# One core, three layers: the first modulation set fetched and used as scale, then shift, and five products of zeros ahead of the first product

## The chip, the core and the metric

The kernel runs on one core of a Trainium2 chip. A time is the device time of one execution in microseconds, and the metric is the median of the runs. A program writes each engine's instructions by hand: TensorE (PE) multiplies, VectorE (DVE), ScalarE (ACT) and GpSimd (POOL) do the rest, SyncE (SP) issues nearly all transfers, 16 DMA engines carry them. Semaphores are the only order between engines.

## What is computed

Two transformer layers and a third block run in sequence on 256 tokens of width 1024, beside a context of 256 tokens. The change touches the first step of the first layer. Cut from the reference:

```python
cond_lat, cond_ctx = silu(c), silu(c_ctx)
sh1, sc1, g1, sh2, sc2, g2 = split(cond_lat @ w_ada[i] + b_ada[i], 6)      # the same for the context
h = rms_norm(x, norm_gain[i, 0]) * (1.0 + sc1) + sh1
y = fftn(h.reshape(b, l, 8, 128), axes=(1, 3), norm='ortho').real          # tokens and 128 channels of a group
x = x + g1 * (y.reshape(b, l, D) @ w_out + b_out)
x = x + g2 * swiglu(rms_norm(x, ...) * (1.0 + sc2) + sh2)
```

Scale multiplies every channel of the spectrum over the tokens; shift is the same for all tokens, and so enters the spectrum only at frequency 0.

## The kernel before

**The front.** Four tiles of tokens (`xnat`) come first. ACT squares them, DVE scales the table of waves by the tokens' norms (`fs`, first tile pair ready at 9.5 us), and `spectrum(c, streams)` on TensorE gives the token spectrum of the 128 channels of chunk c, for stream 0 (latent) and stream 1 (context), in PSUM bank c. `scale_spectrum` (ACT for chunks 0, 2, 4, 6, 7, DVE for 1, 3, 5) multiplies it by gain x (1 + scale) into `Z`; `shift_spectrum` on DVE adds the shift at column 127. `channels(i)` takes the channel DFT of chunks 2i and 2i+1: the even half (columns 127 to 255, with the shift) by `cd`, the odd half (0 to 126) by `sd`. `nyquist(q)` takes the last frequency. ACT copies the results to `yh`, DVE puts the rest into `yl`, and `fnet_chunk(c)`, eight times 27 products, multiplies them by the output weights, split into `whi` (ACT) and `wlo` (DVE) after GpSimd folded them (`fold`).

**The modulation.** Weights come in blocks of 128 x 2048 numbers, one megabyte each, in the order of `STREAM`. A *set* is a stretch of modulation columns. `ada_rows(n, ks)` multiplies the condition by the blocks ks of set n (four products each, into bank 7), ACT copies the sum to `arow` (`arow_of`), `ada_cols(n)` turns it to columns on TensorE, and DVE adds the bias (`mods`) and, for the set of the scale, makes `amod` (`gains`). Set 0 holds shift and scale together: eight blocks of 128 rows and 2048 columns. Set 1 (g1) already comes as four blocks of 256 rows and 1024 columns (`TWO_DEPTHS`), whose turn is four products with a small table in place of four transposes. Set 2 has eight blocks.

**The transfers.** All blocks go through one queue, issued by SP in the order of `STREAM`, each as soon as its slot is free; the first 24 have eight slots (`ring`, `front_ring`). In this text B0 to B7 are the blocks of set 0, B8 is FNet block 0, B9 and B10 set 1, B11 FNet block 1, B12 and B13 set 1, B14 FNet block 2, B15 FNet block 3, B16 to B23 set 2, B24 the first FFN block; the tokens' own f32 copy `xT` (two megabytes) goes behind B14. B16 takes the slot of B8, free when block 0 is folded.

**TensorE's order** is written out by hand: spectrum products with the modulation blocks between them, then channel products, then the eight FNet chunks with the blocks of sets 1 and 2 between them (`MODS`). A product of f32 is two instructions in the trace.

## Time and profile before

| what | value |
|---|---|
| median of 3 runs | 1420.26 us (1420.25 to 1420.28) |
| profiled execution, own time | 1419.94 us |
| its span, first to last instruction | 1418.0 us |
| TensorE busy | 1379.8 us (97%) |
| VectorE, ScalarE, GpSimd busy | 56%, 37%, 5% |
| DMA, mean | 275 GB/s |

The busy share of TensorE is 97% but its ends are modelled, so pauses and pace are read from the timeline. The profiled execution is 0.32 us below the median; differences in the trace are put against its own time and then carried to the median. A row of the timeline gives start, length, engine, line, operation, output and inputs, count, and in brackets the idle time before it with what ended it.

### The profile page before, as it was taken

Reading aid. Unit: us, or ns where it says so; the run is one execution under the profiler, and the core shown is the slowest. Engines: PE = TensorE matmul, PEld = TensorE weight load, DVE = VectorE, ACT = ScalarE, POOL = GpSimd, SP = SyncE. Lnnn points to the kernel's source line nnn. Section 1 sums busy time; section 2 is a strip of 40 time slices with the busy share of each in tenths; the row PEclk is TensorE's granted clock in tenths of the full one; section 3 lists DMA queues with packets and bytes.
Section 4 is the critical chain, followed back from the end, with each engine's and each line's share of the span. In section 5 each row is a group of like instructions: output and inputs, shape, how many; then the busy total and the mean of one; then the engine's idle time right before and its main releaser. Section 6 shows DMA issues by size and latency. Waiting matters only on the chain.

```text
span 1418.0 us, 20093 instructions
## 1 busy us (share of the span) xinstructions
PE 1379.8 (97%) x8038; PEld 994.2 (70%) x8038; DVE 789.1 (56%) x1402; ACT 524.2 (37%) x1099; POOL 75.8 (5%) x74
## 2 busy tenths in 40 slices
PE   7999999999999999999999999999999999999987
PEld 4767887888887998888888998996444444443433
DVE  1978796665666886667788778684212112112113
ACT  2643222223444555445556666852111111111102
POOL 0600000000002141000000000010000000000000
PEclk9999999999999999999999999999999999999999
DMA  9958666764443332013687454478999999999995
GB/s 391 425 220 314 237 249 256 267 241 174 167 175 119 149 129 81 31 60 117 264 340 318 150 208 178 179 305 324 425 432 428 430 430 428 429 432 429 430 427 224
DMA packets 48130, 390.42 MB, mean 275 GB/s; under 512 B 5256, under 2 KB 6552, under 8 KB 9376
## 3 DMA queue, kind: packets, MB, share of 16 engines
q1 hardware_dynamic: 47408, 387.70, 68.1%
q8 instruction: 66, 1.08, 0.3%
q10 hardware_dynamic: 624, 1.37, 0.2%
q14 instruction: 32, 0.26, 0.1%
HBM read 388.01 MB, written 1.05 MB: 274 GB/s over the span
## 4 chain that ended last, share of the span: by engine, by line
PE 85%; DMA 8%; DVE 3%; ACT 2%; issue 1%; SPq 0%; DVEq 0%; ACTq 0%
PE twin L966 41%; PE twin L1627 19%; DMA ring<-in_wblk 6%; PE twin L1064 5%; PE twin L1065 3%; PE twin L1701 2%; DMA front_ring<-in_wblk 2%; PE twin L1610 2%; PE twin L1010 2%; PE twin L1480 2%; PE twin L1305 1%; PE twin L1241 1%; PE twin L1265 1%; DVE wlo L2388 1%; PE twin L886 1%
## 5 line engine op out<-in xcount | busy, mean ns | idle before, releaser
L2388 DVE TENSOR_TENSOR wlo<-ring,whi 128x512 fp32r<-128x512 f32 (+1 forms) x392 | 254.4, 697 | 64.7 <-ACT whi L1820 61.7
L1820 ACT ACTIVATE whi<-ring 128x512 fp32r<-128x512 f32 (+1 forms) x392 | 216.8, 611 | 106.7 <-PE twin L966 86.4
L966 PE MATMUL twin<-H,whi 128*128 128x512 f32 x700 | 216.3, 390 | 0.1
L966 PE MATMUL twin<-hsp,whi 128*128 128x512 f32 (+1 forms) x704 | 172.5, 337 | 1.8 <-DVE hsp L2587 0.9
L1627 PE MATMUL twin<-ring,xg 128*64 128x512 f32 x696 | 158.3, 597 | 8.4 <-DMA ring<-in_wblk 8.0
L966 PEld LDWEIGHTS twin<-H,whi 128*128 128x128 f32 x700 | 130.8, 188 | 30.1 <-issue 2.5
L966 PE MATMUL twin<-H,wlo 128*128 128x512 f32 x350 | 136.2, 389 | 0.0
L966 PEld LDWEIGHTS twin<-hsp,whi 128*128 128x128 f32 x704 | 120.7, 190 | 17.0 <-DVE wlo L2388 1.7
L1064 PE MATMUL twin<-H,whi 128*128 128x512 f32 x350 | 124.2, 400 | 0.5 <-DVE H L2485 0.2
L966 PE MATMUL twin<-hsp,wlo 128*128 128x512 f32 (+1 forms) x352 | 118.3, 336 | 0.0
L1627 PEld LDWEIGHTS twin<-ring,xg 128*64 128x64 f32 x696 | 48.0, 137 | 97.0 <-issue 88.2
L1627 PE MATMUL twin<-ring,xT 128*64 128x512 f32 x456 | 102.0, 595 | 2.5 <-DMA ring<-in_wblk 2.0
L3174 DVE TENSOR_TENSOR rst<-rst,twin 128x512 f32<-128x512 f32 x16 | 11.0, 688 | 166.4 <-issue 161.2
L1065 PE MATMUL twin<-H,wlo 128*128 128x256 f32 x350 | 98.3, 281 | 0.0
L966 PE MATMUL twin<-whi,Hh 128*128 128x256 f32 x304 | 88.3, 291 | 0.0
L966 PE MATMUL twin<-wlo,Hh 128*128 128x256 f32 x304 | 85.9, 283 | 0.0
L966 PE MATMUL twin<-whi,Hl 128*128 128x256 f32 x304 | 85.9, 283 | 0.0
L3189 DVE SCALAR_TENSOR_TENSOR outs<-twin,tiny,outs 128x512 fp32r<-128x512 f32 x32 | 24.0, 751 | 104.6 <-ACT outs L2282 52.8
L1064 PEld LDWEIGHTS twin<-H,whi 128*128 128x128 f32 x350 | 65.8, 188 | 17.6 <-DVE H L2485 0.6
L2587 DVE TENSOR_TENSOR hsp<-hid,hsp 128x512 fp32r<-128x512 f32 (+1 forms) x88 | 49.1, 563 | 50.5 <-ACT hsp L1928 50.5
L1928 ACT ACTIVATE hsp<-hid 128x512 fp32r<-128x512 f32 (+1 forms) x88 | 45.5, 524 | 84.6 <-PE twin L966 84.6
L1627 PEld LDWEIGHTS twin<-ring,xT 128*64 128x64 f32 x456 | 32.1, 137 | 62.4 <-issue 62.3
(428 smaller groups left out, 2375.6 us busy)
## 6 DMA issues: line engine op xcount, KB each, us to landing
ring<-in_wblk SPq DMA_DIRECT2D x213, 1024.0 KB, 6.1
ring<-in_wblk SPq DMA_DIRECT2D x56, 2048.0 KB, 30.6
front_ring<-in_wblk SPq DMA_DIRECT2D x12, 1024.0 KB, 19.1
small<-in_wblk SPq DMA_DIRECT2D x10, 1024.0 KB, 26.4
tmp<-in_wblk SPq DMA_DIRECT2D x9, 1024.0 KB, 23.8
ring<-in_wblk SPq DMA_DIRECT2D x12, 512.0 KB, 18.8
xnat<-in_xnat SPq DMA_DIRECT2D x4, 512.0 KB, 6.7
xT<-in_xin SPq DMA_DIRECT2D x1, 2048.0 KB, 23.4
```

The lines of the kernel that those rows point to most:

```text
L966: t = e.matmul(out, a, b, start=start and n == 0, stop=stop and n == 2)
L1010: e.matmul(out[:, r], ws[x][:, k, m * P:(m + 1) * P], y[:, i, r], start=k == 0 and n == 0, stop=k == KC - 1 and n == 2, skip_group_check=True)
L1064: e.matmul(b[:, :].rearrange("p (x n) -> p x n", x=2), w[0], FHB[1][:, :, k, :], start=start, stop=stop, skip_group_check=True)
L1065: return e.matmul(b[:, 0:L], w[1], FH[1][0][:, k, :], start=False, stop=stop, skip_group_check=True)
L1480: t = e.matmul(wout_bank(b, m)[:, m * L:(m + 1) * L], ws[i][:, k, m * P:(m + 1) * P], XM[j][:, k, :], start=k == 0 and (m == 0 or b == 3) ...
L1610: t = e.matmul(gather_bank(q, j)[:, i * 256:(i + 1) * 256], h2[n % 2][:, n // 2, c * P:(c + 1) * P], Gs[:, n // 2, :], start=n == 0, stop= ...
L1627: t = e.matmul(like(out[64 * i:64 * i + 64, :], rows), lhs(kcs + kk, i), rows, start=start and kk == 0, stop=stop and kk == 3)
L1701: t = e.matmul(acc(c), osp[:, part_, c * P:(c + 1) * P], Sw[:, p % 2, :], start=p == 0 and part_ == 0 and c % 2 == 0, stop=p == NP - 1 and ...
L1820: e.activation(hi, w, ACT.Copy).then_inc(*s_hi.up(m, h))
L1928: e.activation(hsp[:, k % nsp, 0, 0:n], hid[:, k, 0:n], ACT.Copy).then_inc(*s_hph.up(layer, half, k))
L2388: e.tensor_tensor(lo, w, hi.bitcast(F32), ALU.subtract).then_inc(*s_lov.up(m, h))
L2587: e.tensor_tensor(hsp[:, k % nsp, 1, 0:n], hid[:, k, 0:n], hsp[:, k % nsp, 0, 0:n].bitcast(F32), ALU.subtract).then_inc(*s_hpl.up(layer, h ...
```

## The change

The four blocks of scale columns (256 rows, 1024 columns each) now come first, as set 0, the four of the shift columns follow, as a set of its own named "shift" with bank 4 for its rows. Both are turned as set 1 is. ACT's and DVE's scaling of Z waits for set 0 alone. The products of the channel DFT are split: the odd halves wait for the scaled Z, the even halves for the shifted one. Spectrum 4 goes first on TensorE, since bank 4 is wanted for the shift's rows. The late blocks of sets 1 and 2, and the turn of set 1, are placed behind other chunks. GpSimd first clears `rst`, and TensorE multiplies it by itself five times into bank 6, which nobody reads, before its first real product. The host lays the blocks out accordingly. The counts of semaphores that follow from it are left out below.

```diff
@@ -93,12 +93,12 @@
...
 WEIGHED.update({(2, 1 + i): (("fin", 1, 2 * i + 4), 2 * i + 4) for i in range(7)})
-PE_ROWS = {0: range(8), 1: range(4), 2: range(8), 6: range(2), 7: range(1), 8: range(1)}
-ADA0 = {0: (0, 2), 1: (2, 1), 2: (3, 2), "g2": (5, 1)}
-ORDER = [0, 1, 2, "g2", 3, 4, 5, 6, 7, 8]
+PE_ROWS = {0: range(4), "shift": range(4), 1: range(4), 2: range(8), 6: range(2), 7: range(1), 8: range(1)}
+ADA0 = {0: (1, 1), "shift": (0, 1), 1: (2, 1), 2: (3, 2), "g2": (5, 1)}
+ORDER = [0, "shift", 1, 2, "g2", 3, 4, 5, 6, 7, 8]
 BEFORE = dict(zip(ORDER[1:], ORDER[:-1]))
-MOD_STREAMS = {n: 2 if n in (0, 1, 2, "g2", 3) else 1 for n in ORDER}
-TWO_DEPTHS = (1, "g2")
+MOD_STREAMS = {n: 2 if n in (0, "shift", 1, 2, "g2", 3) else 1 for n in ORDER}
+TWO_DEPTHS = (0, "shift", 1, "g2")
 G2 = 4
@@ -474,7 +476,7 @@
...
         def modulated(layer, s, chunk6):
-            return s_mod.at(3 * layer + chunk6 // 2 if layer else (0, 0, 1, 2, 2, "g2")[chunk6], s)
+            return s_mod.at(3 * layer + chunk6 // 2 if layer else ("shift", 0, 1, 2, 2, "g2")[chunk6], s)
@@ -495,8 +497,8 @@
...
         s_a0 = signal("fnet_scales", [(0,)])
-        s_d1 = signal("dft_tokens", [(c,) for c in range(KC)])
-        ACT_SCALED, DVE_SCALED = (0, 2, 4, 6, 7), (1, 3, 5)
+        s_d1 = signal("dft_tokens", [(c,) for c in (4, 0, 1, 2, 3, 5, 6, 7)])
+        ACT_SCALED, DVE_SCALED = (4, 0, 2, 6, 7), (1, 3, 5)
         s_za = signal("spectrum_scaled_act", [(c,) for c in ACT_SCALED])
@@ -635,7 +637,10 @@
...
         def turned_rows(n):
-            return bank[{0: 7, 6: 5}.get(n, 6)]
+            return bank[{0: 7, "shift": 4, 6: 5}.get(n, 6)]
+
+        def rows_bank(n):
+            return bank[4 if n == "shift" else 7]
@@ -872,19 +879,21 @@
...
             def ada_rows(n, ks):
-                layer, s = SETS[n]
+                layer, s = (0, 0) if n == "shift" else SETS[n]
                 for k in ks:
-                    tag = ("ada", layer, s, k)
+                    tag = ("ada", layer, s, k + 4 if n == "shift" else k)
                     w = block_of(tag)
                     e.wait_ge(*landed(tag))
-                    if k == 0 and n:
-                        e.wait_ge(*s_arow.at(n - 1))
+                    if k == 0 and n == "shift":
+                        e.wait_ge(*s_za.at(4))
+                    elif k == 0 and n:
+                        e.wait_ge(*s_arow.at(BEFORE[n]))
                         if n == 1:
...
                     for g in range(4):
-                        depth = 2 * k + g // 2 if n == 1 else k
-                        t = e.matmul(bank[7][32 * g:32 * g + 32, :], cact[:, 1 if layer == 2 else 0, depth, :], w[:, g * 512:(g + 1) * 512],
-                                     start=k == 0, stop=k == (3 if n == 1 else 7), skip_group_check=layer == 2)
+                        depth = 2 * k + g // 2 if n in TWO_DEPTHS else k
+                        t = e.matmul(rows_bank(n)[32 * g:32 * g + 32, :], cact[:, 1 if layer == 2 else 0, depth, :], w[:, g * 512:(g + 1) * 512],
+                                     start=k == 0, stop=k == (3 if n in TWO_DEPTHS else 7), skip_group_check=layer == 2)
                     t.then_inc(*s_adam.up(n, k))
@@ -972,7 +981,7 @@
...
                     for t2 in range(2):
-                        if c == 0:
+                        if c == 4:
                             e.wait_ge(*s_fs.at(2 * s + t2))
@@ -980,12 +989,17 @@
...
-            def channels(i):
-                e.wait_ge(*s_dc.at(2 * i + 1))
-                for table, r, n0, n1 in ((cd, EVEN, 127, 256), (sd, ODD, 0, 127)):
-                    for j in range(2):
-                        t = e.matmul(streams(spectrum_bank[i][64 * j:64 * j + 64, r]), table, Z[:, 2 * i + j, :, n0:n1], start=True, stop=True)
-                t.then_inc(*s_d2.up(i))
+            def channels(i, r):
+                if r == ODD:
+                    for c in (2 * i, 2 * i + 1):
+                        e.wait_ge(*(s_za if c in ACT_SCALED else s_zv).at(c))
+                else:
+                    e.wait_ge(*s_dc.at(2 * i + 1))
+                table, n0, n1 = (sd, 0, 127) if r == ODD else (cd, 127, 256)
+                for j in range(2):
+                    t = e.matmul(streams(spectrum_bank[i][64 * j:64 * j + 64, r]), table, Z[:, 2 * i + j, :, n0:n1], start=True, stop=True)
+                if r == EVEN:
+                    t.then_inc(*s_d2.up(i))
@@ -1016,43 +1030,50 @@
...
-            for c in range(4):
+            e.wait_ge(*s_zero.at("warm"))
+            for _ in range(5):
+                e.matmul(bank[6][:, :], rst[:, 0, 0:P], rst[:, 0, :], start=True, stop=True)
+            for c in (4, 0, 1, 2, 3):
                 spectrum(c, (0,))
+            spectrum(4, (1,))
+            e.wait_ge(*s_cond.at("c2"))
+            ada_rows(0, (0,))
             spectrum(0, (1,))
-            e.wait_ge(*s_cond.at("c2"))
-            ada_rows(0, range(2))
             spectrum(1, (1,))
+            ada_rows(0, (1,))
+            spectrum(2, (1,))
             ada_rows(0, (2,))
-            spectrum(2, (1,))
+            spectrum(3, (1,))
+            spectrum(5, (0,))
             ada_rows(0, (3,))
-            spectrum(3, (1,))
-            spectrum(4, (0,))
-            ada_rows(0, (4,))
-            spectrum(4, (1,))
-            ada_rows(0, (5,))
-            spectrum(5, (0,))
-            ada_rows(0, (6,))
             spectrum(5, (1,))
-            ada_rows(0, (7,))
-            spectrum(6, (0,))
             e.wait_ge(s_cons, 16)
             ada_cols(0)
-            spectrum(6, (1,))
-            spectrum(7)
-            channels(0)
-            channels(1)
+            spectrum(6)
+            spectrum(7, (0,))
+            ada_rows("shift", (0,))
+            spectrum(7, (1,))
+            ada_rows("shift", (1, 2))
+            channels(0, ODD)
+            ada_rows("shift", (3,))
+            channels(1, ODD)
+            ada_cols("shift")
+            channels(2, ODD)
+            channels(3, ODD)
+            channels(0, EVEN)
+            channels(1, EVEN)
             nyquist(0)
-            channels(2)
+            channels(2, EVEN)
             ada_rows(1, range(1))
-            channels(3)
+            channels(3, EVEN)
             nyquist(1)
             ada_rows(1, range(1, 2))
-            MODS = {0: (1, range(2, 4)), 3: (2, range(1)), 4: (2, range(1, 3)), 5: (2, range(3, 5)), 6: (2, range(5, 6))}
+            MODS = {0: (1, range(2, 3)), 1: (1, range(3, 4)), 3: (2, range(1)), 4: (2, range(1, 2)), 5: (2, range(2, 4)), 6: (2, range(4, 6))}
             for c in range(KC):
...
                     ada_rows(*MODS[c])
-                if c == 1:
+                if c == 2:
                     ada_cols(1)
@@ -1823,7 +1844,7 @@
...
                     e.wait_ge(*s_adat.at(BEFORE[i]))
-                e.activation(arow[:, :], bank[7][:, :], ACT.Copy).then_inc(*s_arow.up(i))
+                e.activation(arow[:, :], rows_bank(i)[:, :], ACT.Copy).then_inc(*s_arow.up(i))
@@ -1884,6 +1905,7 @@
...
                 scale_spectrum(c)
+            arow_of("shift")
             for i in range(4):
@@ -1903,7 +1925,7 @@
...
                 e.activation(streams(tmp[:, c % 4, :])[:, :, 0:129:128], streams(even)[:, :, 0:129:128], ACT.Identity, bias=col("fb", c)).then_inc(*s_fna.up(c, "ends"))
-                if c == 0:
+                if c == 1:
                     arow_of(1)
@@ -2308,6 +2330,7 @@
         def pool(e):
+            e.memset(rst[:, 0, :], 0.0).then_inc(*s_zero.up("warm"))
             e.memset(cact[:, :, :, :], 0.0).then_inc(*s_zero.up("cact"))
@@ -2541,14 +2564,11 @@
...
             e.wait_ge(*s_a0.at(0))
-            scale_spectrum(1)
-            shift_spectrum(0)
-            shift_spectrum(1)
-            scale_spectrum(3)
-            shift_spectrum(2)
-            shift_spectrum(3)
-            scale_spectrum(5)
-            for c in range(4, KC):
+            for c in DVE_SCALED:
+                scale_spectrum(c)
+            mods("shift")
+            e.wait_ge(*s_mod.at("shift", 1))
+            for c in range(KC):
                 shift_spectrum(c)
@@ -3323,9 +3343,10 @@
...
             m = w["w_ada_2"][0] if t[1] == 2 else w["w_ada"][t[1]]
-            if t[1] == 0 and t[2] in (1, 3):
-                a = 2048 if t[2] == 1 else 5120
-                wblk[n] = m[t[3] * 2 * P:(t[3] + 1) * 2 * P, a:a + BW // 2].reshape(2, P, BW // 2).transpose(1, 0, 2).reshape(P, BW)
+            if t[1] == 0 and t[2] != 2:
+                a = {0: 0 if t[3] >= 4 else 1024, 1: 2048, 3: 5120}[t[2]]
+                k = t[3] % 4
+                wblk[n] = m[k * 2 * P:(k + 1) * 2 * P, a:a + BW // 2].reshape(2, P, BW // 2).transpose(1, 0, 2).reshape(P, BW)
             else:
...
                 wblk[n] = m[t[3] * P:(t[3] + 1) * P, a:a + BW]

```

Three places of the engines' order, each row an instruction group of the program (line, operation, output and inputs, output shape, count of products). TensorE from its first product on, before:

```order
L977 MATMUL twin<-fs,xnat 128x256 x10
L886 MATMUL twin<-ring,small 32x512 x8
L977 MATMUL twin<-fs,xnat 128x256 x2
L886 MATMUL twin<-ring,small 32x512 x4
L977 MATMUL twin<-fs,xnat 128x256 x2
```

and in the changed kernel:

```order
L1035 MATMUL twin<-rst 128x512 x5
L986 MATMUL twin<-fs,xnat 128x256 x12
L895 MATMUL twin<-ring,small 32x512 x4
L986 MATMUL twin<-fs,xnat 128x256 x4
L895 MATMUL twin<-ring,small 32x512 x4
```

Five products of zeros stand first; the first modulation block comes two spectrum products later and alone. (L977 and L986 are `spectrum`, L886 and L895 `ada_rows`.) TensorE from the last blocks of set 0 to the channel products, before:

```order
L886 MATMUL twin<-front_ring,small 32x512 x4
L977 MATMUL twin<-fs,xnat 128x256 x2
L916 MATMUL twin<-cons,small 128x128 x4
L977 MATMUL twin<-fs,xnat 128x256 x6
L987 MATMUL twin<-Z,dft 64x258 x2
L987 MATMUL twin<-Z,dft 64x254 x2
L987 MATMUL twin<-Z,dft 64x258 x2
L987 MATMUL twin<-Z,dft 64x254 x2
L992 MATMUL twin<-Z,dft 32x258 x4
```

and in the changed kernel:

```order
L923 MATMUL twin<-cons,small 128x8 x4
L986 MATMUL twin<-fs,xnat 128x256 x6
L895 MATMUL twin<-front_ring,small 32x512 x4
L986 MATMUL twin<-fs,xnat 128x256 x2
L895 MATMUL twin<-front_ring,small 32x512 x8
L1000 MATMUL twin<-Z,dft 64x254 x2
L895 MATMUL twin<-front_ring,small 32x512 x4
L1000 MATMUL twin<-Z,dft 64x254 x2
L923 MATMUL twin<-cons,small 128x8 x4
L1000 MATMUL twin<-Z,dft 64x254 x4
L1000 MATMUL twin<-Z,dft 64x258 x4
L1006 MATMUL twin<-Z,dft 32x258 x4
```

The turn (L916, now L923) of the scale stands ahead of the shift blocks, a second turn behind them, and odd channel products (64x254) lie around it. DVE from the modulation to the first split, before:

```order
L2400 TENSOR_TENSOR mod<-twin,cols 128x16 x2
L2468 SCALAR_TENSOR_TENSOR amod<-mod,cols 128x8 x2
L2532 TENSOR_SCALAR Z<-twin,amod 128x256 x2
L2541 SCALAR_TENSOR_TENSOR Z<-mod,Z 128x2 x2
L2532 TENSOR_SCALAR Z<-twin,amod 128x256 x2
```

and in the changed kernel:

```order
L2423 TENSOR_TENSOR mod<-twin,cols 128x8 x2
L2491 SCALAR_TENSOR_TENSOR amod<-mod,cols 128x8 x2
L2555 TENSOR_SCALAR Z<-twin,amod 128x256 x6
L2423 TENSOR_TENSOR mod<-twin,cols 128x8 x2
L2564 SCALAR_TENSOR_TENSOR Z<-mod,Z 128x2 x8
```

The three scalings stand together, and all eight shifts behind the second `mod`.

## Rows read from the trace of the kernel before

**Rows 1.** The page, part 4: the chain that ended last, by engine

```profile
PE 85%; DMA 8%; DVE 3%; ACT 2%; issue 1%; SPq 0%; DVEq 0%; ACTq 0%
```

**Rows 2.** Chain of waits, 0 to 200 us: start, us, what

```profile
6.43 25.16 DMA front_ring<-in_wblk
...
33.76 0.45 PE twin L916 x4
...
35.34 3.75 ACT Z L1881 x10
...
90.62 46.63 PE twin L966 x204
```

**Rows 3.** Timeline of TensorE, first 80 us

```profile
9.54 7.21 PE L977 MATMUL twin<-fs,xnat 128*128 128x256 f32 x20 [9.54 <-DVE fs L2509]
...
31.63 1.06 PE L886 MATMUL twin<-front_ring,small 128*32 128x512 f32 x8 [0.82 <-DMA front_ring<-in_wblk]
...
43.85 0.39 PE L1010 MATMUL twin<-yh,whi 128*128 128x258 f32 x1
...
45.41 0.39 PE L1010 MATMUL twin<-yh,whi 128*128 128x258 f32 x1 [0.20 <-DVE yl L2555]
...
47.75 1.92 PE L886 MATMUL twin<-front_ring,small 128*32 128x512 f32 x16
49.60 0.39 PE L1010 MATMUL twin<-yh,whi 128*128 128x258 f32 x1
...
52.94 0.96 PE L914 MATMUL twin<-cons,small 128*128 128x8 f32 x8
53.75 0.37 PE L1010 MATMUL twin<-yh,whi 128*128 128x258 f32 x1
...
60.39 1.06 PE L886 MATMUL twin<-ring,small 128*32 128x512 f32 x8
...
79.63 1.02 PE L924 MATMUL twin<-hid,cons 128*128 128x512 f32 x2
```

**Rows 4.** Busy time from 15 to 80: engines, then PEclk, DMA share, GB/s

```profile
15.00:80.00 65.00, 63.97 (x474) 42.25 (x473) 38.73 (x75) 25.57 (x56) 25.92 (x16) 1.00 1.01 424
```

**Rows 5.** Spectrum products (L977) in two stretches: PE, PEld, PEclk, DMA share, GB/s

```profile
9.50:14.80 5.30, 5.26 (x12) 4.21 (x13) 1.00 1.02 426
14.80:16.60 1.80, 1.80 (x9) 1.37 (x7) 1.00 1.00 423
```

**Rows 6.** SP's issue of B16, then of B24, each with its time to landing

```profile
38.93 0.33 SPq L841 DMA_DIRECT2D ring<-in_wblk  x1
...
DMA to landing us min/median/max: 19.5/19.5/19.5
...
65.03 0.43 SPq L841 DMA_DIRECT2D ring<-in_wblk  x1
...
DMA to landing us min/median/max: 13.1/13.1/13.1
```

**Rows 7.** Timelines of ACT (one row) and DVE around the modulation

```profile
32.77 0.60 ACT L1826 ACTIVATE small<-twin 128x512 f32<-128x512 f32 x1 [18.38 <-PE twin L886]
...
34.24 0.26 DVE L2400 TENSOR_TENSOR mod<-twin,cols 128x16 f32<-128x16 f32 x2 [18.59 <-PE twin L916]
34.44 0.86 DVE L2468 SCALAR_TENSOR_TENSOR amod<-mod,cols 128x8 f32<-128x8 f32 x2
...
38.47 0.82 DVE L2541 SCALAR_TENSOR_TENSOR Z<-mod,Z 128x2 f32<-128x2 f32 x4
```

**Rows 8.** Timeline of GpSimd: first clear, fold of blocks 0 and 3

```profile
0.73 0.52 POOL L2311 MEMSET small<- 128x512 f32 x1 [0.29 <-POOLq L3296]
...
33.93 4.97 POOL L2327 TENSOR_TENSOR fold<-ring 128x512 f32<-128x512 f32 x4 [31.53 <-DMA ring<-in_wblk]
...
56.11 8.52 POOL L2327 TENSOR_TENSOR fold<-front_ring 128x512 f32<-128x512 f32 x4 [1.33 <-DMA front_ring<-in_wblk]
```

**Rows 9.** Busy time of the stretch 960 to 980, PEclk third from the end

```profile
960.00:980.00 20.00, 19.57 (x130) 16.34 (x130) 10.61 (x41) 9.13 (x19) 0.00 (x0) 0.91 0.78 306
```

More of the change, by code:

```diff
@@ L459, in program @@
         s_cond = signal("conditions_ready", [("c0",), ("c2",)])
-        s_zero = signal("cleared", [("cact",), ("wny",), ("eps",), ("pick",), ("lx",), ("sT",)])
+        s_zero = signal("cleared", [("warm",), ("cact",), ("wny",), ("eps",), ("pick",), ("lx",), ("sT",)])
         events = []
@@ L465, in program @@
                 events.append([("sum", "g2"), ("rows", "g2")])
+            if n == 1:
+                events += [[("shift", k)] for k in range(3)] + [[("shift", 3), ("rows", "shift")]]
             mine = [[(n, k)] for k in PE_ROWS.get(n, ())] + [[("sum", n)]] * (layer > 0)
@@ L785, in used @@
                         e.wait_ge(*s_adv.at("g2", tag[3]))
+                    elif tag[1:3] == (0, 0) and tag[3] >= 4:
+                        e.wait_ge(*s_adam.at("shift", tag[3] - 4))
                     else:
```

## The prediction

> **What bounds the kernel now.** The page comes first: TensorE holds 85% of the chain that ended last, DMA 8% [rows 1]. The change touches the first 60 us only, so the chain of waits of that stretch is next. It hangs on one transfer until 31.59 us, block B7, the eighth of the first modulation set; from the first layer's FFN on it is TensorE [rows 2]. TensorE's own timeline shows what lies between [rows 3]: products without a pause from 9.54 to 30.81, a pause of 0.82 for B7, and then again no pause until chunk 0 of the FNet output product at 43.85, in which it waits once more (45.41, for the low part of the spectrum). A normal chunk takes 3.34 (49.60 to 52.94), chunk 0 takes 3.90 (43.85 to 47.75). So TensorE is the bound from 31.6 on, and up to there it runs only 0.82 ahead of the transfers. Underneath, the DMA engines are full: their share is 1.01 of the stretch from 15 to 80 [rows 4], so no transfer of it can land sooner; only their order can change, and each set keeps its eight megabytes.
>
> One more thing is in TensorE's front. Its first 12 matmul instructions (each product of f32 is two) take 5.26 us, the next 9 take 1.80, though the forms are the same and the granted clock reads 1.00 in both [rows 5]. Start to start that is 0.43 against 0.216 us: the engine ran at 1.2 GHz when it came out of idling and at 2.4 GHz from 14.8 us. What this costs is 12 x (0.427 - 0.216) = 2.53 us. In the kernel before most of it would not pay back: all but 0.82 us of TensorE's lead is waiting for B7 anyway if it comes early.
>
> **The change part by part.**
>
> *Scale first.* B7, now the last shift block, lands at 31.6 as before [rows 2]. B3, now the last scale block, is four blocks of 1.05 MB ahead of it, at 424 GB/s [rows 4] some 9.9 us, so at about 21.7. TensorE's own pace in the new order, from rows 3 at full clock (four spectrum instructions 0.86 and up to 0.2 for the change of kind, a modulation block 1.0, a turn of eight 0.81): it starts at 9.54, has done 24 spectrum instructions at 14.9, scale blocks and their neighbours at 23.8, the turn at 25.7, and reaches the last shift block at about 32.9. That is 1.3 later than B7 lands. So the wait for B7 (0.82) is gone, and TensorE alone sets the time. The scaling of Z, which began 3.7 us after B7's products before (31.63 to 35.34) [rows 2, 3], begins at about 27, on ACT and DVE, beside spectrum products.
>
> *The second turn.* One turn of 4 instructions, 0.45 [rows 2], becomes two of 8; one such turn takes 0.81 (52.94 to 53.75) [rows 3]. Added on TensorE: 2 x 0.81 - 0.45 = 1.17 us. The weight blocks themselves cost the same: eight blocks, four products each. Behind the shift blocks a new chain stands: copy of the rows on ACT, turn, mod on DVE (0.26), eight shifts of Z (four took 0.82, so 1.6 in all); the copy itself takes 0.60 [rows 7]. TensorE covers the copy with the odd products of pair 1 and the mod and the first shifts with the odd products of pairs 2 and 3 (1.0 us). The old chain had these steps too, with amod (0.86) and the scaling between them; I take 0.3 us of waits left, bounds 0 (all covered) and 1.1 (copy and mod bare, 0.6 + 0.26 and their handing over).
>
> *Channel products in halves.* The same instructions; the odd half needs no shift. No cost beyond a seam or two. The yh, whi, yl, wlo chain on ACT and DVE starts about 1.8 earlier and TensorE arrives at chunk 0 about 2 earlier; the folded weights of chunk 0 are ready at 38.9 (33.93 + 4.97) [rows 8] and do not bind. The 0.56 us that chunk 0 loses now (3.90 - 3.34) goes, since the Z scaling no longer fills both engines up to 39 us; bounds 0 and 0.56.
>
> *Five products of zeros.* They need a memset of 512 columns, 0.52 us from 0.73 on [rows 8], so they start at about 1.3. At the low clock one instruction of 512 columns takes twice 0.427, so ten take 8.5 us at most; if the clock rises after the same 5.3 us of work as in the trace, at 6.6, they end at 8.3, before 9.54, when the scaled waves of the first tile are there. They then cost nothing, and the main products start at 2.4 GHz: 2.53 us less. The pause between them and 9.54 is 1.2 us; the nearest one in the rows is the 0.82 at 30.8, behind which a modulation block takes 1.06 like the one at 60.39 [rows 3]. The other clears on GpSimd come 0.5 later, and nobody waits for them before 13 us.
>
> The Trainium skill, "TensorE: Matmul & The Clock Gate", Part 1, says the default state of the clock is the throttled one and that activity of the engine releases it; rows 5 agree. By that rule zeros count as work like any other, and the sum stays. The same part warns that the point of the rise varies from run to run; then some of the 2.53 us could be lost in one execution, by the next step less than half a microsecond of time.
>
> *Sum up to the end of chunk 3.* Before, the modulation block behind chunk 3 starts at 60.39. Off it: 0.82 + 2.53 + 0.56 = 3.91; on it: 1.17 + 0.3 = 1.47. The two late blocks of set 1 and its turn are only moved within this stretch. TensorE would arrive at 60.39 - 2.44 = 57.95.
>
> *What is late next.* There it needs B16, the first block of set 2. Its DMA is issued at 38.93, when the fold of FNet block 0 frees its slot, and lands 19.5 later, at 58.43 [rows 6]. The fold waits for B8's landing (33.93), not for TensorE, so the issue time does not move, and neither does the landing with full DMA engines. So TensorE waits about 0.5 us and starts B16 at 58.47 in place of 60.39: **1.92 us** are left. Behind it the new list spreads the blocks of set 2 over later chunks: at 424 GB/s a block of 1.05 MB follows every 2.5 us, so B17 lands at about 60.9 and is taken after chunk 4 at about 62.8, B18 and B19 land at 63.4 and 65.9 and are taken after chunk 5 at about 67.2. None binds. DVE and ACT have slack behind chunk 6, and chunk 7 ends 1.92 sooner than 79.63 [rows 3]. B24, the first FFN block, lands at 65.03 + 13.1 = 78.1 [rows 6]; ACT would want it at 78.4, so it just does not bind.
>
> *To the end.* From there on TensorE carries the chain, and the transfers wait for slots that TensorE, ACT and DVE free, up to the expert stage, whose fill also hangs on them. I see nothing that gives the time back: the shift passes whole. Profiled execution: 1419.94 - 1.92 = 1418.02; the median of the runs stands 0.32 above it, so 1420.26 - 1.92 = **1418.3**.
>
> **The rivals.**
>
> *The zeros do not lift the clock* (slower). The mechanism: zeros, or the pause of 1.2 us behind them, leave the engine at 1.2 GHz until about 14.8. Then 2.53 us come back, and the ten instructions, all at 0.855, end at 9.85, which delays the first real product by 0.3. TensorE arrives behind chunk 3 at 57.95 + 2.83 = 60.8 and is 0.4 later than before: 1420.7. It decides from 2.44 us of loss on. For it: nothing in the rows shows products of zeros. Against it: the rise comes while the engine works, whatever is in it.
>
> *B16 does not hold* (faster still). If it lands sooner or TensorE's sum is right and the block is there, 2.44 us: 1417.8. Against it: the DMA share of 1.01.
>
> *The low parts hold.* Folding one block took 4.97 us when DVE mostly read PSUM and 8.52 when DVE worked from SBUF beside it [rows 8]. DVE now splits weights earlier, beside the fold of block 1. If chunk 2 or chunk 6 finds its low weights missing by 1 us, what is left is about 0.9: 1419.4. The Trainium skill, "GPSIMD Engine Reference", section "Key points", says that GpSimd shares its SBUF interfaces with VectorE and contends with instructions of two SBUF inputs; rows 8 agree.
>
> *The clock at a later stage.* The granted clock is 0.91 in the stretch 960 to 980 [rows 9]. A start 1.9 us sooner may lose or gain one stretch at half clock somewhere, priced by the front's at 2.5: 1420.8 or 1415.8.
>
> **How the numbers follow.** Forecast (1417.8 to 1418.8, by the waits of 0 to 1.1 and B16's hold): 0.60. B16 not holding 0.08, low parts 0.12, zeros 0.09, later clock stretch 0.09 (half each way), anything worse 0.02. The range leaves out the later gain and half of the slow ends: 1417.3 to 1420.7. This kernel's measurement can tell about 0.2%, 2.84 us. Faster than that (below 1417.42) needs the later gain, or B16 early by more than 0.5 with no wait left: 0.08. Slower than 1423.1 needs zeros and a later loss together: 0.03. Within: 0.89.
>
> **What would show it.** Products of the first spectrum chunks at 0.216 from 9.5 on; no pause before the last shift block; the last shift block's products at about 33; chunk 0 at about 41.7 and 3.4 long; a pause of about 0.5 before the block behind chunk 3, which starts at 58.4 to 58.5; the first FFN products 1.9 sooner. It would be wrong if those first products still took 0.43, if B16 landed elsewhere than at 58.4, or if the gap between the two traces changed anywhere behind 90 us.

## The result and the profile after

| what | before | changed |
|---|---|---|
| median of the runs taken side by side (14 each) | 1419.74 us (1418.13 to 1421.23) | 1421.59 us (1419.06 to 1424.53) |
| ratio to before, 95% interval | | 1.0018 (1.0011 to 1.0025) |
| profiled execution, own time | 1419.94 us | 1424.53 us |
| its span | 1418.0 us | 1422.3 us |
| start of the first layer's FFN products (chain) | 90.62 us [rows 2] | 93.33 us |

The changed kernel is slower: by 1.9 us between the two medians, by 2.6 by the ratio, with an interval of 1.6 to 3.5. The forecast was 1.9 us faster. The shares of the chain that ended last look much as before [rows 1] and do not tell why; the timelines of the first 70 us do.

**The front does what was forecast, with one exception.** TensorE's timeline of the changed kernel (start, length, engine, line, operation, output and inputs, shape, count, idle time before it and what ended it):

```profile
1.31 6.17 PE L1035 MATMUL twin<-rst 128*128 128x512 f32 x10 [1.31 <-POOL rst L2333]
9.31 5.45 PE L986 MATMUL twin<-fs,xnat 128*128 128x256 f32 x24 [1.83 <-DVE fs L2532]
...
32.61 1.06 PE L895 MATMUL twin<-front_ring,small 128*32 128x512 f32 x8
...
37.70 0.66 PE L1000 MATMUL twin<-Z,dft 128*64 128x258 f32 x4 [0.57 <-DVE Z L2564]
...
42.53 0.39 PE L1024 MATMUL twin<-yh,whi 128*128 128x258 f32 x1
...
46.15 1.06 PE L895 MATMUL twin<-front_ring,small 128*32 128x512 f32 x8
```

The 24 spectrum instructions take 5.45 us, 0.22 each, where the first 12 of before took 0.43 each [rows 5]: the ten instructions of zeros take 6.17 us, 0.85 from start to start at first (1.2 GHz) and 0.43 at the end (2.4 GHz), and the real ones find the 2.4 GHz level, in spite of 1.83 us of idling between them. The last shift block is worked on at 32.61 with no pause ahead of it. Behind it the spectrum waits 0.57 us for the eight shifts of DVE (L2564), and chunk 0 starts at 42.53, 1.3 earlier than before [rows 3], where I had 41.7.

**Then the gain is lost at one place.** TensorE again, from the turn of set 1 on. The first fence is the changed kernel, the second before, where the turn stood one chunk earlier [rows 3]:

```profile
54.87 0.96 PE L923 MATMUL twin<-cons,small 128*128 128x8 f32 x8
...
59.08 1.06 PE L895 MATMUL twin<-ring,small 128*32 128x512 f32 x8
62.55 0.56 PE L1024 MATMUL twin<-yh,whi 128*128 128x258 f32 x1 [2.40 <-DVE wlo L2411]
62.90 0.42 PE L1024 MATMUL twin<-yl,whi 128*128 128x258 f32 x1
...
67.47 1.07 PE L895 MATMUL twin<-ring,small 128*32 128x512 f32 x8
```

```profile
61.38 0.39 PE L1010 MATMUL twin<-yh,whi 128*128 128x258 f32 x1
```

At 59.08 TensorE is 1.31 ahead of before (60.39). Chunk 4 should follow at 60.1; it waits 2.40 us for the low part of its weights, starts at 62.55, 1.17 *behind* before (61.38), and its first products, some 15 of them, take 0.215 us from start to start (62.90 to 63.12 and so on), where those of chunk 0 take 0.12. Here is why DVE is late, changed kernel, timelines of DVE and of GpSimd:

```profile
55.86 0.24 DVE L2423 TENSOR_TENSOR mod<-twin,cols 128x8 f32<-128x8 f32 x2 [3.79 <-PE twin L923]
56.14 5.75 DVE L2550 SCALAR_TENSOR_TENSOR xT<-tmp,mod,xT 128x256 f32<-128x256 f32 x4
61.81 2.48 DVE L2411 TENSOR_TENSOR wlo<-fold,whi 128x512 fp32r<-128x512 f32 x4
```

```profile
55.98 5.63 POOL L2350 TENSOR_TENSOR fold<-front_ring 128x512 f32<-128x512 f32 x4 [1.73 <-DMA front_ring<-in_wblk]
```

and the same of DVE before:

```profile
54.74 1.67 DVE L2527 SCALAR_TENSOR_TENSOR xT<-tmp,mod,xT 128x256 f32<-128x256 f32 x4
56.33 2.49 DVE L2388 TENSOR_TENSOR wlo<-fold,whi 128x512 fp32r<-128x512 f32 x4
```

DVE adds the FNet result times g1 to `xT` (L2550), and that needs the modulation of set 1, hence its turn. Before, the turn came behind chunk 1, DVE began the four additions at 54.74 and was in the last of them when GpSimd came to fold block 3 (56.11, [rows 8]). Now the turn comes behind chunk 2, the additions begin at 56.14, and the fold began at 55.98, when its block had landed. The additions begin 1.4 us apart in place of 0.4, one with each fold instruction. Behind them in DVE's queue stand the four `wlo` of chunk 4, for which TensorE waits. Before, the order of arrival was the other way round, and it was GpSimd that was held up: 8.52 us for the fold [rows 8], which nobody on the chain waits for; it takes 5.63 now.

The chain of waits of the changed kernel tells the same in one line each (start, us, what):

```profile
56.14 5.75 DVE xT L2550 x4
...
62.55 4.64 PE twin L1024 x24
...
93.33 6.77 PE twin L975 x28
```

**A second loss on top.** Busy time of the changed kernel (PE, PEld, DVE, ACT, POOL, then PEclk, DMA share, GB/s):

```profile
60.00:65.00 5.00, 2.60 (x15) 2.45 (x12) 4.96 (x9) 0.63 (x1) 1.61 (x2) 0.76 1.01 424
65.00:70.00 5.00, 5.00 (x38) 4.03 (x37) 4.34 (x10) 4.09 (x10) 0.00 (x0) 0.90 1.01 426
...
930.00:935.00 5.00, 5.00 (x22) 4.60 (x22) 2.41 (x4) 2.60 (x8) 1.47 (x2) 0.50 0.56 197
```

Behind the 2.40 us of waiting the granted clock falls (0.76, then 0.90), and chunk 4 with its Nyquist products takes 4.92 us from its start to the block behind it (62.55 to 67.47). In the kernel before it takes 3.40, and in a second trace of the changed kernel (e7, below) 3.43. That is 1.5 us more, so the stretch costs 1.31 + 1.17 + 1.52 = 4.0 us in this execution, and the FFN starts 2.71 late. The offset between the two traces stays at about 2.7 up to 920 us and jumps to 5.7 where the granted clock is 0.50 (930 to 935; 1.00 there before). It falls by 1.0 where the kernel before has a half-clock stretch of its own (at 967), and the spans end 4.3 apart.

### The profile page after: what moved, and what is told of

Read it like the earlier page. It is cut to its first block, busy times and chain, and to the rows that moved or that the text cites. A ratio compares the mean times of both kernels' runs of the same rounds, so it can differ in the third digit from the quotient of the medians.

```text
span 1422.3 us, 20149 instructions
## 1 busy us (share of the span) xinstructions
PE 1389.6 (98%) x8060; PEld 999.3 (70%) x8060; DVE 792.3 (56%) x1404; ACT 525.2 (37%) x1100; POOL 72.7 (5%) x75
## 3 DMA queue, kind: packets, MB, share of 16 engines
q8 instruction: 66, 1.08, 0.3%
HBM read 388.01 MB, written 1.05 MB: 274 GB/s over the span
## 4 chain that ended last, share of the span: by engine, by line
PE 87%; DMA 6%; DVE 4%; ACT 2%; issue 1%; SPq 0%; DVEq 0%; ACTq 0%
PE twin L975 41%; PE twin L1648 19%; DMA ring<-in_wblk 6%; PE twin L1085 5%; PE twin L1086 3%; PE twin L1722 2%; PE twin L1631 2%; PE twin L1024 2%; PE twin L1501 2%; PE twin L895 1%; PE twin L1326 1%; PE twin L1262 1%; PE twin L986 1%; PE twin L1286 1%; DVE wlo L2411 1%
```

## The experiments

Two theories. **A**, the collision: DVE's additions lose their place ahead of GpSimd's fold because the turn of set 1 was moved; the waiting and all the loss come from that. **B**, the new front itself: less slack between fetched blocks, DVE and ACT behind because of the second turn and the eight shifts, so that the loss would stay wherever the turn is. (The expectations below use B for other rivals, and each says which: in e1 stretches of half clock at later stages, in e3 no effect at all, in e7 a wait that does not come back.) Each ratio is uncertain by some 1.3 us either way, so the verdicts rest on the start of the first layer's FFN products in the trace, and the ratios are read beside it. Three groups (the first four, the next three, the last two) have each their own runs of before beside them.

**e1_turn_back.** The changed kernel with the turn of set 1 and its blocks back where they were.

```
-            MODS = {0: (1, range(2, 3)), 1: (1, range(3, 4)), 3: ...
+            MODS = {0: (1, range(2, 4)), 3: ...
-                if c == 2:
+                if c == 1:
                     ada_cols(1)
...
-                if c == 1:
+                if c == 0:
                     arow_of(1)
```

> The changed kernel with one part undone: both late blocks of set 1 stand behind chunk 0 and its turn behind chunk 1, as before the change. Theory A (collision): in the changed kernel DVE's four additions to xT start at 56.14 us, the moment GpSimd starts to fold block 3, and take 5.75 us in place of 1.67; the low weights of chunks 4 and 5 come late for it, TensorE waits 2.4 us and runs chunk 4 partly at 1.2 GHz. With the turn back the additions start at 53.7 (xT lands then) and are over before the fold: no wait before chunk 4, FFN's long run of products starts at about 88.7 to 89.2 (90.6 before, 93.3 changed), time 1.5 to 2 us below the kernel before. Theory B (the loss is not in the front but in stretches of half clock at later stages, which come or stay away by chance of the start): the median stays within 1 us of the changed kernel's, 1.5 to 2 above before, wherever the FFN starts.

Measured: 1418.33 us against 1419.08 of before, ratio 0.9997 (0.9988 to 1.0006). DVE's timeline, TensorE's block behind chunk 3, and the chain:

```profile
53.60 2.24 DVE L2550 SCALAR_TENSOR_TENSOR xT<-tmp,mod,xT 128x256 f32<-128x256 f32 x4 [0.42 <-DVE mod L2423]
...
58.86 1.06 PE L895 MATMUL twin<-ring,small 128*32 128x512 f32 x8
...
89.09 11.07 PE twin L975 x47
```

The additions take 2.24 us (the first of them 1.05, beside the last fold instruction of block 2) and are over at 55.8, TensorE does not wait for chunk 4, and the FFN starts at 89.09: 1.53 sooner than before and 4.24 sooner than in the changed kernel. The front alone would have left the wait there. Half clock at later stages would have left the median 1.5 to 2 above before; it is 0.75 below, less than the 1.5 to 2 expected by A and inside what the ratio leaves open.

**e2_fold_waits.** The turn stays late; GpSimd is told to wait with the fold of block 3 until the four additions are through.

```
+                    if b == 3:
+                        e.wait_ge(*s_fnx.at(1, 1))
```

> The changed kernel, its order untouched, but GpSimd folds block 3 only when DVE has finished the first two chunks' additions to xT. Theory A: the additions take 1.7 us (56.1 to 57.8) again, the low weights of block 2 are there at about 60.3, TensorE waits at most 0.3 us before chunk 4 and the FFN starts at about 89; time 1 to 2 us below the kernel before. Rival C (the additions are slow for another reason, such as the landing of xT or full transfers into SBUF): they still take over 4 us and the time stays at the changed kernel's. Rival D (the fold is needed at once): the wait is only moved to chunk 6, and the gain is under 1 us.

Measured: 1418.38 us against 1419.08, ratio 0.9994 (0.9985 to 1.0003). DVE, GpSimd, chain:

```profile
56.36 1.67 DVE L2552 SCALAR_TENSOR_TENSOR xT<-tmp,mod,xT 128x256 f32<-128x256 f32 x4
...
58.20 8.06 POOL L2352 TENSOR_TENSOR fold<-front_ring 128x512 f32<-128x512 f32 x4 [3.71 <-DVE xT L2552]
...
89.54 10.60 PE twin L975 x45
```

With the turn as late as in the changed kernel, the additions take 1.67 again as soon as GpSimd is not beside them, and the FFN starts 1.08 sooner than before. So it is the meeting that costs, not the late turn as such. The fold begins 2.2 late and takes 8.06, and nobody on the chain waits for it: rival D of the expectation, a wait moved to chunk 6, falls too, since TensorE has no pause ahead of chunk 6 (69.95).

**e3_before_late_turn.** The kernel before, with nothing of the change but the turn of set 1 behind chunk 2.

```
-                if c == 1:
+                if c == 2:
                     ada_cols(1)
```

> The kernel before with one part of the change alone: the turn of set 1 behind chunk 2 in place of chunk 1. TensorE does the same products. Theory A: DVE's four additions start at about 57.9, inside the fold of block 3 (56.1 on), and take 4 to 6 us; low weights of chunk 4 come at 64 or later, TensorE waits 2 to 3 us there: FFN start 92.5 to 94, time 2 to 4 us above before. Theory B: nothing that can be measured, within 0.5 us of before.

Measured: 1420.85 us against 1419.08, ratio 1.0010 (1.0001 to 1.0019). DVE, TensorE's chunk 4, chain:

```profile
55.87 4.83 DVE L2527 SCALAR_TENSOR_TENSOR xT<-tmp,mod,xT 128x256 f32<-128x256 f32 x4
...
62.43 0.39 PE L1010 MATMUL twin<-yh,whi 128*128 128x258 f32 x1 [2.55 <-DVE wlo L2388]
...
91.70 8.34 PE twin L966 x35
```

One changed number makes the old kernel slower and shows the same wait (2.55 for 2.40) and the same stretched additions (4.83). The FFN starts 1.08 late, less than the 1.9 to 3.4 expected, because TensorE was 1.6 ahead here at the block behind chunk 3 (58.81 against 60.39): it took B7 0.8 earlier in this execution, and chunk 0 took 3.42 in place of 3.90. Behind the wait it was late by 1.08: 2.7 us went. Without that head start the additions would have begun later still, so 1.1 us is, by this argument, the least that the one line costs. One thing does not fit a plain order of arrival: the first addition began at 55.87, 0.12 *ahead* of the fold (55.99), and was through in 0.48; the other three were caught (1.5 each).

**e4_before_zeros.** The kernel before with the clear and the five products of zeros, and nothing else.

```
+            e.wait_ge(*s_zero.at("warm"))
+            for _ in range(5):
+                e.matmul(bank[6][:, :], rst[:, 0, 0:P], rst[:, 0, :], start=True, stop=True)
...
+            e.memset(rst[:, 0, :], 0.0).then_inc(*s_zero.up("warm"))
```

> The kernel before with the memset and the five products of zeros alone. The prediction said that TensorE's lead over the eighth block is waited away: the first spectrum products run at 0.216 us from 9.5 on, the pause before the last block of set 0 grows from 0.82 to about 3.3 us, chunk 0 starts at 43.85 as before, and the time is that of the kernel before within 0.3 us. Rival: a pause of 3.3 us before the last block lets the clock fall again (the granted clock under 1.00 behind it, products at 0.43), and the time is 1 to 3 us above before.

Measured: 1419.39 us against 1419.08, ratio 0.9999 (0.9989 to 1.0009). TensorE's timeline and the chain:

```profile
9.51 4.58 PE L977 MATMUL twin<-fs,xnat 128*128 128x256 f32 x20 [1.00 <-DVE fs L2513]
...
15.96 1.06 PE L886 MATMUL twin<-ring,small 128*32 128x512 f32 x8 [0.88 <-DMA ring<-in_wblk]
...
29.14 1.06 PE L886 MATMUL twin<-front_ring,small 128*32 128x512 f32 x8 [1.20 <-DMA front_ring<-in_wblk]
...
90.65 9.45 PE twin L966 x40
```

The 20 instructions take 4.58 in place of 7.21 [rows 3], and the 2.6 us are waited away again. I had expected one pause of 3.3 before B7; there are five smaller ones (0.88, 0.30, 0.30, 1.20, 0.21), and the granted clock stays at 1.00 through them. In the old order the zeros are worth nothing (+0.03 at the FFN); the prediction had said that most would not pay back.

**e5_one_shift.** e1, and the eight shifts of Z as one instruction of 128 x 16 in place of eight of 128 x 2.

```
-            def shift_spectrum(c):
...
-                e.scalar_tensor_tensor(Z[:, c, :, 127:128], shift, math.sqrt(2.0), Z[:, c, :, 127:128], ALU.mult, ALU.add).then_inc(*s_dc.up(c))
+            def shift_spectrum():
...
+                shift = mod[:, 0, :].rearrange("p (s x) -> p s x", s=2)[:, :, 0:KC]
+                at_zero = Z[:, :, :, 127:128].rearrange("p c s n -> p s (c n)")
+                e.scalar_tensor_tensor(at_zero, shift, math.sqrt(2.0), at_zero, ALU.mult, ALU.add).then_inc(*s_dc.up(0))
```

> The version with the turn of set 1 back behind chunk 1, and the eight additions of the shift to Z joined in one instruction of 128 x 16 numbers. Theory A (a DVE instruction that reads two operands in SBUF waits for the GpSimd instruction that runs, so each of a row of short ones pays up to one fold of 1.27 us): the eight cost 3.3 us in the runs so far, one costs at most 1.4, the wait of TensorE before the even products (0.57) and the short ones behind it go, chunk 0 starts about 0.8 to 1.2 sooner than at 42.6, and the block B16, landing at 58.4, takes back all but 0.3 to 0.5 of it: FFN start 88.6 to 88.8, time 1.5 to 2.5 us below before. Rival E (the additions are slow because each waits for its own predecessor, with GpSimd or without): one instruction costs 0.15 to 0.3 and chunk 0 starts 1.5 or more sooner.

Measured: 1417.94 us against 1419.55, ratio 0.9987 (0.9979 to 0.9996): faster than before. DVE, TensorE, chain:

```profile
35.75 0.73 DVE L2563 SCALAR_TENSOR_TENSOR Z<-mod,Z 128x16 f32<-128x16 f32 x1
...
41.73 0.39 PE L1024 MATMUL twin<-yh,whi 128*128 128x258 f32 x1
...
58.45 1.06 PE L895 MATMUL twin<-ring,small 128*32 128x512 f32 x8 [0.43 <-DMA ring<-in_wblk]
...
88.71 11.49 PE twin L975 x49
```

This is the trace that the prediction described, but of another kernel, with two parts of the change made otherwise: chunk 0 at 41.73 (41.7), a wait of 0.43 for B16 behind chunk 3 (0.5), its products at 58.45 (58.47), the FFN 1.91 sooner (1.92). Rival E of the expectation, that the shifts are slow with GpSimd or without, falls with e6, where eight of them take 0.66 with the fold over.

**e6_no_zeros.** e1 without the five products of zeros; the clear stays.

```
-            for _ in range(5):
-                e.matmul(bank[6][:, :], rst[:, 0, 0:P], rst[:, 0, :], start=True, stop=True)
```

> The version with the turn of set 1 back, without the five products of zeros. The prediction's step: with scale first TensorE has no lead left, so the half clock of the first products now costs its full 2.5 us: first spectrum products at 0.43, the last shift block taken at about 35 in place of 32.6, chunk 0 at about 45, the block behind chunk 3 at about 61.3 with no wait for its landing. Its FFN start is then 91.3 to 92 (89.1 with zeros, 90.6 before), and the time 0.7 to 1.5 us above before. If the rival holds that the zeros are worth nothing here as they were in the kernel before, FFN start stays at 89.1 to 89.5.

Measured: 1420.22 us against 1419.55, ratio 1.0004 (0.9995 to 1.0012). TensorE's first rows, DVE's shifts, the chain:

```profile
9.58 8.10 PE L986 MATMUL twin<-fs,xnat 128*128 128x256 f32 x24 [9.58 <-DVE fs L2530]
...
35.54 1.06 PE L895 MATMUL twin<-front_ring,small 128*32 128x512 f32 x8
...
38.69 0.66 DVE L2562 SCALAR_TENSOR_TENSOR Z<-mod,Z 128x2 f32<-128x2 f32 x8
...
91.05 9.01 PE twin L975 x38
```

The FFN starts 1.96 later than in e1 and 0.43 later than before. In the new order the zeros are needed: without them TensorE reaches the last shift block at 35.54. Of the 2.9 us lost there (32.61 in the changed kernel, 32.64 in e1), about 1.0 comes back, a little more than expected (91.3 to 92). One source is the shifts: they fall behind GpSimd's fold of block 0 here (it ends at 38.2) and take 0.66 us, where they take 3.26 beside it in the changed kernel.

The second meeting happens here too, although the turn is early. DVE:

```profile
55.17 2.72 DVE L2548 SCALAR_TENSOR_TENSOR xT<-tmp,mod,xT 128x256 f32<-128x256 f32 x4
57.82 5.84 DVE L2409 TENSOR_TENSOR wlo<-fold,whi 128x512 fp32r<-128x512 f32 x4
```

The fold of block 3 begins at 56.04 and catches the fourth addition and three of the `wlo`. TensorE does not wait for them: it comes to chunk 4 at 61.82 here, and behind chunk 3 it is 1.96 later than in e1 (60.82 against 58.86), the same as at the FFN. So the 1.96 is the zeros' worth and holds nothing of this meeting.

**e7_changed_again.** The changed kernel, unchanged, beside e5 and e6.

> The changed kernel as it is, beside the others on one chip. Theory A: the wait of about 2.4 us before chunk 4 recurs in every execution, since it hangs on GpSimd's fold beginning before DVE's additions. What the clock does behind it may differ: either chunk 4 runs partly at 1.2 GHz (FFN start near 93.3) or not (near 91.7); the stretch at half clock near 930 us of the first trace stays away or stands elsewhere. Theory B: the wait itself is gone in this execution.

Measured: 1422.0 us against 1419.55, ratio 1.0015 (1.0007 to 1.0024), the first result again. Chain, DVE and the window behind the wait:

```profile
56.19 5.72 DVE L2550 SCALAR_TENSOR_TENSOR xT<-tmp,mod,xT 128x256 f32<-128x256 f32 x4
...
60.00:65.00 5.00, 2.63 (x24) 2.44 (x21) 4.97 (x8) 0.63 (x1) 1.63 (x2) 1.00 1.00 421
...
91.84 8.33 PE twin L975 x35
```

The stretched additions and the wait are there again to a few hundredths, the half clock behind it is not: granted clock 1.00, FFN at 91.84 in place of 93.33. So 1.22 us late is what the collision alone leaves of the change, and the other 1.5 of the first trace come with the half clock. That they belong to one execution alone is not shown: the medians stand 1.9 and 2.5 above before, and the granted clock over a whole execution is lower in this kernel (mean of its 26 executions 0.9963, of the 85 of before beside the experiments 0.9974, of e3's 11, with the same wait, 0.9976). Some loss at half clock therefore recurs; where it lies, two traces do not tell.

**e8_late_turn_one_shift.** One question was left: with chunk 0 at 41.7 instead of 42.5, as I had forecast, the additions would begin ahead of the fold. Is it the slow shifts that tip the order over (theory C), or is the late turn bad in itself (D)? The changed kernel with e5's one shift instruction and nothing else.

> The changed kernel with its late turn of set 1, and only the eight shifts of Z made one instruction. In the changed kernel the additions to xT begin 0.16 us behind the fold of block 3 (56.14 and 55.98); with chunk 0 at 41.7 in place of 42.5 they should begin at about 55.3, ahead of the fold by 0.7. Theory C: the slow shifts are what tips the order over. Then DVE, being under way, keeps its lead as before the change (there the fold came 1.37 us into DVE's run): additions in 1.6 to 1.7 us, no wait ahead of chunk 4, B16 waited for until 58.45, FFN products at 88.7, median about 1.9 us below before. Theory D: being ahead by less than a microsecond does not help, the fold gets in after the second addition (in the old kernel with the late turn the fold came 0.12 us after the first addition began and did get in): two additions at 0.4, two at 1.5, additions done at about 59.2, the weights of chunk 4 at about 60.0 to 61, chunk 4 0.4 to 1.5 late, FFN at 89.1 to 90.2.

Measured: 1420.27 us against 1419.29, ratio 1.0008 (0.9999 to 1.0018). DVE, GpSimd, TensorE, chain:

```profile
55.21 2.73 DVE L2550 SCALAR_TENSOR_TENSOR xT<-tmp,mod,xT 128x256 f32<-128x256 f32 x4
57.87 5.82 DVE L2411 TENSOR_TENSOR wlo<-fold,whi 128x512 fp32r<-128x512 f32 x4
...
56.09 6.44 POOL L2350 TENSOR_TENSOR fold<-front_ring 128x512 f32<-128x512 f32 x4 [1.76 <-DMA front_ring<-in_wblk]
...
61.42 0.39 PE L1024 MATMUL twin<-yh,whi 128*128 128x258 f32 x1 [0.72 <-DVE wlo L2411]
...
90.95 9.23 PE twin L975 x39
```

C falls. The additions begin 0.88 ahead of the fold, three of the four take their 0.4 us, the fold gets in ahead of the fourth, and now the four `wlo` of chunk 4 meet it instead: 5.82 us in place of 2.5. TensorE waits inside chunk 4, several times up to 0.7 us each. The FFN starts at 90.95, 0.33 later than before. That is D's mechanism at more than D's price (89.1 to 90.2), since I had let the weights go unhindered. So neither arrival tried with the late turn is a good one: 0.88 ahead of the fold, the weights are caught; 0.16 behind it, all four additions.

**e9_one_shift_again.** e5 unchanged, beside e8.

> The kernel of the run with the turn of set 1 back and one shift instruction, unchanged, beside it. If its gain is not of one chip and one session: FFN products at 88.7 (to 0.2), ratio between 0.998 and 0.9996 again. If the first ratio was luck: 0.9997 or above.

Measured: 1417.72 us against 1419.29, ratio 0.9990 (0.9980 to 0.9999). Chain:

```profile
88.75 11.28 PE twin L975 x48
```

Against e8 it differs in the place of the turn and of one block alone: 2.20 us at the FFN. The gain of e5 is there again, 1.87 us in the trace.

All in one table; the offset is the start of the FFN products against 90.62 of before, the last column the interval of the ratio in microseconds of before's median:

| kernel | offset in the trace | interval of the runs |
|---|---|---|
| changed | +2.71 | +1.6 to +3.5 |
| e7, changed again | +1.22 | +1.0 to +3.4 |
| e1, turn of set 1 back | -1.53 | -1.7 to +0.9 |
| e2, fold waits | -1.08 | -2.1 to +0.4 |
| e3, before with late turn | +1.08 | +0.1 to +2.7 |
| e4, before with zeros | +0.03 | -1.6 to +1.3 |
| e5, e1 with one shift | -1.91 | -3.0 to -0.6 |
| e6, e1 without zeros | +0.43 | -0.7 to +1.7 |
| e8, changed with one shift | +0.33 | -0.1 to +2.6 |
| e9, e5 again | -1.87 | -2.8 to -0.1 |

Every offset lies within the interval of its runs. In all ten traces the offset is still the same at 560 us, to 0.03. Behind that the traces part: e1, e2 and e9 gain 0.9 more between 560 and 900 us, which no run here explains, and stretches at half clock, in other places in each execution, add or take 1 to 3 us. What the first 90 us give or take passes to the end only within what the runs can resolve.

## Why the prediction was wrong

**Where it failed.** The step that failed is "The two late blocks of set 1 and its turn are only moved within this stretch". I counted the turn's own 0.81 us on TensorE, found it unchanged, and did not follow who waits for it: ACT's copy, DVE's `mod`, the four additions to `xT`, and behind them in the same queue the weights of chunk 4. The prediction gives no reason for taking the move as free; all it says of these queues is "DVE and ACT have slack behind chunk 6". At chunk 4 DVE had 1.7 us of additions and 2.5 of weights to do, in a place that it shared with GpSimd's fold. The move delayed the additions by 1.40 (54.74 to 56.14), which put them from just ahead of the fold to just behind its start. Price: 5.75 - 1.67 = 4.1 us on DVE, 2.4 of waiting on TensorE. e1 and e2 remove it by either of its two partners, e3 makes it in the old kernel, e7 repeats it, and e8 shows that the forecast would have failed at this step even with every other term right: +0.33 where I had -1.92.

**The rival that was nearest.** "The low parts hold" was the right mechanism with the right rows (the fold of 4.97 and of 8.52), but I looked for it at chunks 2 and 6, gave it 1 us and a chance of 0.12, and had GpSimd as the one that is slowed. Rows 8 show the direction in which the collision is harmless. The harmful one, DVE held up by a fold that came first, could nearly have been worked out before: the fold of block 3 begins at 56.11 [rows 8]; the turn comes a chunk later, 52.94 + 3.34 [rows 3], less the 2.4 that I had TensorE ahead, so at 53.9 at best; the additions follow 1.27 behind a turn in the changed kernel (54.87 to 56.14), so at 55.2 (55.21 in e8); four of them and four `wlo` are 4.0 us of work (54.74 to 58.74 before), most of it behind 56.1. The Trainium skill, "SBUF — State Buffer", section "Who interferes with whom", says it outright: "Issue order, not op shape, decides who blocks." The traces agree in the main: with DVE ahead, four additions take 1.67 and the fold 8.52; with the fold ahead, it takes 5.63 and the additions 5.75. How far ahead is enough, they answer unevenly (last section).

**The shifts** (a term of the right kind, too small). I had eight at 1.6 us, from four at 0.82 [rows 7], and 0.3 us of waits. They took:

```profile
35.77 3.26 DVE L2564 SCALAR_TENSOR_TENSOR Z<-mod,Z 128x2 f32<-128x2 f32 x8
```

beside this row of GpSimd:

```profile
33.84 4.95 POOL L2350 TENSOR_TENSOR fold<-ring 128x512 f32<-128x512 f32 x4 [30.98 <-DMA ring<-in_wblk]
```

It is the same collision at another place. The new order sets the shifts at 35.8, inside the fold of block 0 (33.84 to 38.8); alone they take 0.66 (e6), as one instruction 0.73 (e5). It put chunk 0 at 42.53 in place of 41.7. Without the other loss it would cost 0.4 us (e1 against e5: 89.09 and 88.71), since B16 holds TensorE 0.43 in e5 anyway. Putting this right alone would not have saved the forecast (e8: +0.33).

**What held.** *The zeros*: the products start at the 2.4 GHz level after ten instructions that ended at 7.5 (I had 8.3) and a pause of 1.83 (1.2); e6 puts their worth in the new order at 1.96, e4 at nothing in the old one. The rival "the zeros do not lift the clock" falls in every trace with them. *B7*: no pause, last shift block at 32.61 (32.9). *The second turn, the halves, chunk 0*: chunk 0 with its Nyquist products takes 3.6 (42.53 to 46.15), inside the bounds of 3.34 and 3.90, though the 0.56 came back only in part. *B16*: lands so that its products start at 58.45 in e5, 58.47 on paper. In the changed kernel TensorE came later than that, at 59.08, and did not wait. *The pass to the end*: unchanged to 560 us, and behind that as said under the table. The gap between the traces did change behind 90 us, which the prediction had named as a sign of being wrong. The sum for the first 60 us gives e5's trace to 0.01 us and e9's to 0.05, and not that of this kernel. That closeness is in part luck: "chunk 0 at about 41.7" does not follow from the sum, which gives 43.85 - 0.82 - 2.53 + 1.17 + 0.3 = 41.97. In e5 TensorE is 0.24 ahead of it there, loses that within the chunks (it would have been at the block behind chunk 3 at 58.02, where the sum has 57.95), and the landing of B16 covers the rest.

**The clock at a later stage** was a rival with 2.5 us either way. It is real, and its places change from execution to execution: the stretch at 930 with 0.50 in the first trace reads 1.00 in e1 and e5. There it costs 3.0 us (offset 2.7 to 5.7), and before's own at 967 costs 1.0. It raises the profiled execution of the changed kernel (1424.53) over its median (1421.59). The median's own step may hold a part of it, as the granted clocks under e7 say. It is not the main part: e7 and e1 differ by 2.75 us at the FFN, e8 and e9 by 2.20, with no half clock in any of the four traces up to there.

## What to carry to other kernels

Moving an instruction on the bounding engine by one stage is not free because its own length is the same: follow its result through the queue of the engine that consumes it, and list what stands behind the consumer. Where VectorE instructions with two SBUF inputs come near a run of GpSimd instructions on the same memory, their order of arrival decides in the main which of the two is held up. Being first by 0.12 or 0.88 us was not enough (e3, e8), so place the whole run that the chain needs clearly ahead, or let the other wait for it as in e2. A row of tiny VectorE instructions is badly exposed: here one strided instruction for all of them cut 3.26 us to 0.73. And products of zeros that lift the clock pay only where TensorE sets the time behind them: 1.96 us in the new order (e6), nothing in the old one (e4).

## What the runs showed that was not expected

- VectorE and GpSimd do not slow each other evenly. Beside a running fold, additions of 128 x 256 take 1.4 to 1.5 us each where four in a row take 1.67 together, one addition per fold instruction, and the fold goes on at nearly its own pace (5.63 for 4.95).
- What happens when GpSimd arrives in the middle of a run of VectorE depends on more than who was first. The fold of block 3 begins when its block lands, at 55.98 to 56.11 in every trace but e2. Where the next instruction in VectorE's queue was then a `wlo` of 128 x 512 (before, e1, e2, e4, e5, e9), the `wlo` went through at their own pace and the first fold instruction took 3.3 to 4.0 us. Where it was an addition of 128 x 256 (the block landed during the first addition in e3, during the third in e6 and e8), the fold got in ahead of it, and until the fold was over every two-input instruction of VectorE waited, the `wlo` too. Whether the kind of instruction or something finer decides was not tried.
- The length of a VectorE instruction hardly matters in it: eight of 128 x 2 take 3.26 us beside the fold (0.66 alone; three of the eight waited, up to 1.24 us each), one of 128 x 16 takes 0.73 (0.37 in e8).
- A wait of about 2.5 us on TensorE was followed by a stretch at half clock in one traced execution of three (changed kernel: granted clock 0.76 and 0.90; e7 and e3: 1.00). It cost 1.5 us. What decides it was not tried.
- The granted clock reads 1.00 over the first real products in both kernels, though they run at 0.43 us in one [rows 5] and 0.22 in the other. For the level of the first microseconds the distance from start to start is the evidence, not that column.
